# GpSimd multiplies the dense stage's products by the gates from the fourth pair of tiles on

## The chip, the cores and the metric

The kernel runs on one core of a Trainium2 chip. Its time is the device time of that core in microseconds. The core has five engines with a queue of their own: TensorE (PE, the matmuls; its weight loads are shown as PEld), VectorE (DVE), ScalarE (ACT), GpSimd (POOL) and SyncE (SP, which issues DMAs here). They meet only at semaphores, and each works through its own instructions in order.

## The reference, cut to what matters

One layer of a decoder: attention and a short convolution, then a mixer over 16384 experts of one neuron each. Only the mixer (`_peer`) is touched. For each of 512 tokens it picks 8 x 16 experts by key scores, and then:

```
ug = take(u, experts)                     # 128 rows of 2048 per token
vg = take(v, experts)
act = gelu(einsum("tkd,td->tk", ug, h)) * gates
out = einsum("tk,tkd->td", act, vg)
```

All is float32.

## The kernel before, in words

The 512 tokens are four blocks of 128. For block 0 the kernel gathers the chosen rows of u and v. For blocks 1, 2 and 3 it computes gelu(u h) for all experts (the sweep, 128 tiles of 128 experts) and keeps the products in HBM. The gates of blocks 2 and 3 are scattered into the same HBM array, so that `grid` holds for each expert 256 products and beside them 256 gates, which are zero where a token did not choose the expert.

The stage that follows the sweep, called the dense stage here, does two things at once.

- **The dense sum, blocks 2 and 3.** For each tile of 128 experts PE multiplies the weighed products by the tile of v. Both are float32 and split into a high and a low part, so a tile is 24 matmuls of 128x512. Tiles go in pairs: `grid_rows` holds four tiles (two pairs) and there are two such buffers. For a pair, VectorE multiplies products by gates in place (`weigh_pair`, L1930, one 128x512 instruction), ScalarE makes the high part (`split_pair`, L1346), VectorE the low part (`rest_pair`, L1935). For a tile, ScalarE makes the high part of v (`split_v`, L1342) and VectorE the low part (`rest_v`, L1925). PE waits for `v_lo_ready` at each tile and for `a_lo_ready` at each even one.
- **The gathered sum, block 1.** For each of 128 slots c GpSimd gathers one row of v per token into one of eight buffers (`gather_v`, L986), an indirect DMA of 1 MB, and VectorE adds it with its factor (`accumulate`, L1974). From slot 8 on the gather waits until sum c-7 is done (sum c-3 for the last eight: `LATE_AHEAD`). The factors of a head (16 slots) come from 16 tiny indirect DMAs (`fetch_product`, L975), issued one head ahead.

The order on the two engines is written out by hand. VectorE at tile n: `rest_v(n)`; at even n `weigh_pair(n//2+1)`; at odd n `rest_pair(n//2+1)`; then the sums `added(n)` to `added(n+1)`, which is 16 sums in 15 tiles from tile 7 on. GpSimd: the 16 fetches of head 0, the gathers of slots 2 to 7, and then for each head h eight gathers (slots 8 to 15 of the head) with two fetches for head h+1 behind each, followed by the first eight gathers of head h+1 with nothing between. Head 7 has no fetches. ScalarE at tile b: `split_v(b)`, and at odd b `split_pair` of the next pair behind it.

The line of before's `dense` that the change takes out, with its neighbours:

```
rest_v(tile, b)
if tile < TILES - 2 and b % 2 == 0:
    weigh_pair(pair + 1)
if tile < TILES - 2 and b % 2 == 1:
    rest_pair(pair + 1)
for c in range(added(tile), added(tile + 1)):
    accumulate(c)
```

Of the kernel before, what the change touches and what calls it, by code (L numbers as in the profile page):

```python
# [30 lines left out]
ALU = mybir.AluOpType  # L31
# [20 lines left out]
TOPK = 16  # L52
SWEPT = SEQ - P
SWEPT_BLOCKS = TB - 1
TILES = N_EXPERTS // P
# [11 lines left out]
PAIRS = TILES // 2  # L67
GROUP = 4
GROUP_RING = 2
FIRST_ADDED = 7  # L70
LATE_AHEAD = RING // 2
QUAD = 32
QUADS = P // QUAD
NEAR, FAR = 0, 1
# [117 lines left out]
def decoder_layer(nc, x, attn_norm_g, w_in, q_norm_g, k_norm_g, lambda_q1, lambda_k1, lambda_q2, lambda_k2,  # L192
                  subln_g, conv_w, w_out, ffn_norm_g, peer_w_q, peer_subkeys, peer_u, peer_v, out):
    ctx = ExitStack()
    with ctx:
        def sb(name, shape, dt=F32):
            return ctx.enter_context(nc.sbuf_tensor(name, shape, dt))

        def sem(name):
            return ctx.enter_context(nc.semaphore(name))  # L200

        def sems(name, n):
            return [sem(f"{name}{i}") for i in range(n)]
# [16 lines left out]
        def at(name, kb, shape, dt=F32):  # L220

            return nc.alloc_sbuf_tensor_at(name, shape, dt, offset=base + int(kb * KB))
# [37 lines left out]
        far_rows = at("far_rows", 128, [P, D])  # L260
        far_turned = at("far_turned", 136, [P, QUADS, KT, QUAD])
        v_row = [at(f"v_row{i}", 120 + 8 * i, [P, D]) for i in range(2)]
# [36 lines left out]
        def late_sb(name, shape, dt=F32):  # L299
# [5 lines left out]
        seg_rows = [nc.alloc_sbuf_tensor_at("near_rows", [P, D], F32, offset=late), far_rows]  # L305
        seg_turned = [nc.alloc_sbuf_tensor_at("near_turned", [P, QUADS, KT, QUAD], F32, offset=late + 8 * KB), far_turned]
        half_rows = [nc.alloc_sbuf_tensor_at(f"half_rows{i}", [P, D // HALVES], F32, offset=late + 4 * KB * i) for i in range(2)]
        half_rows.append(at("half_rows2", 124, [P, D // HALVES]))
        half_turned = [nc.alloc_sbuf_tensor_at(f"half_turned{i}", [P, QUADS, KT // HALVES, QUAD], F32,
                                               offset=late + 8 * KB + 4 * KB * i) for i in range(2)]  # L310
        half_turned.append(at("half_turned2", 140, [P, QUADS, KT // HALVES, QUAD]))
        wo0_hi = nc.alloc_sbuf_tensor_at("wo0_hi", [P, QUARTER, CHUNK], F32R, offset=late)
# [36 lines left out]
        pair = sb("pair", [P, 2, TOPK], U32)  # L349
# [24 lines left out]
        def pair_of(pair, first):  # L374

            half = pair % (GROUP // 2)
            return grid_rows[pair // (GROUP // 2) % GROUP_RING][:, 2 * half:2 * half + 2, first:first + GRID]

        def products_of(pair):
            return pair_of(pair, 0)  # L380

        def gates_of(pair):
            return pair_of(pair, GRID)
# [20 lines left out]
        ps_key_scores = [ps[:, 7 - c, :].rearrange("p (t n) -> p t n", t=TB) for c in range(2)]  # L404
        uT_rows = [u_tile[b][:, :].rearrange("p (a k e) -> p k a e", a=QUADS, e=QUAD) for b in range(2)]
        ps_uT = [ps[:, 2 * i:2 * i + 2, :].rearrange("p b (k e) -> p (b k) e", k=4) for i in range(2)]
# [97 lines left out]
        v_tile_used = sem("v_tile_used")  # L504
        group_in = sems("group_in", GROUP_RING)
        weights_ready = sem("weights_ready")
        a_hi_ready = sem("a_hi_ready")
        a_lo_ready = sem("a_lo_ready")
        dense_done = sem("dense_done")
# [38 lines left out]
        def halves_turned(j, i):  # L548

            return 4 * (NEAR_HEADS + 1) + 2 * (HALVES_A_HEAD * j + i)  # L550

        @nc_block.sync
        def _(sp):
# [15 lines left out]
            def next_half(j, i):  # L570

                (tile, _), half = half_place(j, i)
                sp.wait_ge(seg_ready[NEAR], halves_turned(j, i) - 2 * TURNED_SINCE[i])
                load_half(half_of_head(i), tile, half)
# [264 lines left out]
        def _(pool):  # L839
# [88 lines left out]
            def slot(t, h, s):  # L928
                return bass.IndirectOffsetOnAxis(ap=experts[:, t, h * TOPK + s:h * TOPK + s + 1], axis=0)
# [19 lines left out]
            for i in range(PEER_HEADS):  # L949
                pool.wait_ge(chosen, TB * i + 1)  # L950
                for b in range(TOPK):
                    c = TOPK * i + b
# [8 lines left out]
                    for h, n in scatters_beside(c):  # L961
                        if n == 0:
# [7 lines left out]
                            in_=gates[:, 2 + d, col:col + 1], in_offset=None, compute_op=ALU.add)\  # L970
                            .then_inc(grid_done, 16)

            def fetch_product(h, s):
                col = h * TOPK + s
                pool.indirect_dma_start(  # L975
                    out=dots[:, s:s + 1], out_offset=None, in_=products_one,
                    in_offset=bass.IndirectOffsetOnAxis(ap=cells[:, col:col + 1], axis=0))\
                    .then_inc(cells_in, 16)

            def gather_v(h, s):  # L980
                c = h * TOPK + s
                ahead = RING if c < TILES - RING else LATE_AHEAD
                if c >= RING:
                    pool.wait_ge(v_used, c - ahead + 1)
                    pool.sem_inc(past_wait, 1)
                pool.indirect_dma_start(out=v_ring[s % RING][:, :], out_offset=None, in_=v_table,  # L986
                                        in_offset=slot(1, h, s)).then_inc(v_in[s % RING], 16)
# [8 lines left out]
            for s in range(TOPK):  # L996
                fetch_product(0, s)
            for s in range(2, RING):
                gather_v(0, s)
            for h in range(PEER_HEADS):  # L1000
                if h < PEER_HEADS - 1:
                    pool.wait_ge(acts_ready, h + 1)
                for s in range(RING, TOPK):
                    gather_v(h, s)
                    if h < PEER_HEADS - 1:
                        fetch_product(h + 1, 2 * (s - RING))
                        fetch_product(h + 1, 2 * (s - RING) + 1)
                if h < PEER_HEADS - 1:
                    for s in range(RING):
                        gather_v(h + 1, s)  # L1010

        @nc_block.scalar
        def _(act):
# [327 lines left out]
                nc.scalar.activation(v_hi[b % 2][:, :], v_raw(h, b), ACT.Copy).then_inc(v_hi_ready, 1)  # L1342

            def split_pair(pair, i):
                act.wait_ge(weights_ready, pair + 1)
                nc.scalar.activation(a_hi[i % 2][:, :, :], products_of(i), ACT.Copy).then_inc(a_hi_ready, 1)  # L1346

            split_u(0, 0, 0)
# [33 lines left out]
        def _(dve):  # L1382
# [476 lines left out]
            def dot(c):  # L1859
                b = c % TOPK  # L1860
                dve.wait_ge(u_in[c % 2], 16 * (c // 2 + 1))
                v.tensor_tensor_reduce(out=u_row[c % 2][:, :], in0=u_row[c % 2][:, :], in1=h_rows[:, 0, :],  # L1862
                                       scale=1.0, scalar=0.0, op0=ALU.mult, op1=ALU.add,
                                       accum_out=dots0[:, b:b + 1]).then_inc(u_used[c % 2], 1)

            def add(c):
                b = c % TOPK
                dve.wait_ge(acts0_done, c + 1)
                dve.wait_ge(v0_in[c % 2], 16 * (c // 2 + 1))
                past()  # L1870
                v.scalar_tensor_tensor(out=x_rows[:, 0, :], in0=v_row[c % 2][:, :], scalar=acts0[:, b:b + 1],  # L1871
                                       in1=x_rows[:, 0, :], op0=ALU.mult, op1=ALU.add)\
                    .then_inc(v0_used[c % 2], 1)
                dve.wait_ge(v0_used[c % 2], c // 2 + 1)
# [48 lines left out]
            def rest_v(c, b):  # L1923
                dve.wait_ge(v_hi_ready, c + 1)
                v.tensor_tensor(v_lo[b % 2][:, :], v_raw(c // TOPK, b), v_hi[b % 2][:, :].bitcast(F32),  # L1925
                                ALU.subtract).then_inc(v_lo_ready, 1)

            def weigh_pair(pair):
                dve.wait_ge(group_in[pair // 2 % GROUP_RING], 16 * (pair // 2 // GROUP_RING + 1))
                v.tensor_tensor(products_of(pair), products_of(pair), gates_of(pair), ALU.mult)\  # L1930
                    .then_inc(weights_ready, 1)

            def rest_pair(pair):
                dve.wait_ge(a_hi_ready, pair + 1)
                v.tensor_tensor(a_lo[pair % 2][:, :, :], products_of(pair), a_hi[pair % 2][:, :, :].bitcast(F32),  # L1935
                                ALU.subtract).then_inc(a_lo_ready, 1)
# [37 lines left out]
                v.scalar_tensor_tensor(out=x_one[:, :], in0=v_ring[s % RING][:, :], scalar=acts[:, s:s + 1],  # L1974
                                       in1=x_one[:, :], op0=ALU.mult, op1=ALU.add).then_inc(v_used, 1)

            def added(tile):
                return min(TILES, max(0, (tile - FIRST_ADDED) * TILES // (TILES - 1 - FIRST_ADDED)))

            def dense():  # L1980
                rest_v(1, 1)
                dot(TILES - 1)
                rest_v(2, 2)
                rest_pair(1)
                add(TILES - 1)
                weigh_pair(2)
                for tile in range(3, TILES):
                    pair, b = tile // 2, tile % TOPK
                    rest_v(tile, b)
                    if tile < TILES - 2 and b % 2 == 0:  # L1990
                        weigh_pair(pair + 1)
                    if tile < TILES - 2 and b % 2 == 1:
                        rest_pair(pair + 1)
                    for c in range(added(tile), added(tile + 1)):
                        accumulate(c)
# [376 lines left out]
```

## Time and profile before

| | us |
|---|---|
| median of 3 runs (2933.47 to 2937.99) | 2937.51 |
| the profiled execution | 2933.1 |
| its span, first to last instruction | 2931.0 |
| PE busy in the span | 2879.4 |
| VectorE busy | 2392.2 |
| GpSimd busy | 1672.4 |
| ScalarE busy | 1057.1 |

The span is one execution. The dense stage's matmuls begin at 2184.1 us of it and end a few us before the last instruction. Busy time of an engine is an average over stages; what a change in one stage is worth is read in that stage. A POOL row of an indirect DMA is GpSimd's work to issue it, not the transfer. DMA share is the mean busy share of 16 DMA engines; it can read slightly over 1.

### The profile page before, as it was taken

To read this page: it belongs to the slowest core of one execution; us is meant where nothing else is said; L and a number is where in the kernel's file an instruction comes from. 1 tells how busy PE (TensorE), PEld (TensorE's weight loads), DVE (VectorE), ACT (ScalarE), POOL (GpSimd) and SP (SyncE) were. 2 spreads that over 40 slices of the span, in tenths; PEclk is the share of its full clock that TensorE was granted. 3 is DMA by queue.
4 is the path that set the end of the run, shared out by engine and by line. 5 is a ranking of instruction groups with operands and counts; after the bars stand their busy time and mean duration, and the time that the engine had idled before them with its cause. 6 is when DMAs were issued, how large, how long until landed. Compare 5 with 4: busy or idle time off the path is not lost.

```text
span 2931.0 us, 40438 instructions
## 1 busy us (share of the span) xinstructions
PE 2879.4 (98%) x14769; PEld 2546.0 (87%) x14769; DVE 2392.2 (82%) x3106; ACT 1057.1 (36%) x1375; POOL 1672.4 (57%) x1078
## 2 busy tenths in 40 slices
PE   7999999999999999999999999999999999999999
PEld 6888777778899999999999999999997777877787
DVE  6555888855679898988989898899777998999898
ACT  4121433341334343434333343444233333333333
POOL 1000565500116778765766666576868888887762
PEclk9999999999999999999999999999999999999999
DMA  8998999979978998999999999999999999999999
GB/s 300 328 354 275 307 307 297 302 277 335 308 261 304 328 355 307 347 322 342 335 314 348 310 341 329 332 341 365 335 367 394 411 419 416 418 421 419 419 416 375
DMA packets 332718, 1010.00 MB, mean 345 GB/s; under 512 B 65748, under 2 KB 182496, under 8 KB 247072
## 3 DMA queue, kind: packets, MB, share of 16 engines
q1 hardware_dynamic: 181648, 523.28, 48.0%
q0 software_dynamic: 113344, 454.44, 42.8%
q10 hardware_dynamic: 37584, 30.43, 3.2%
q8 instruction: 84, 1.38, 0.2%
q14 instruction: 58, 0.48, 0.0%
HBM read 881.01 MB, written 127.01 MB: 344 GB/s over the span
## 4 chain that ended last, share of the span: by engine, by line
PE 68%; DVE 11%; issue 6%; DMA 6%; POOL 6%; ACT 1%; ACTq 0%; DVEq 0%; SPq 0%; POOLq 0%
PE ps L2026 21%; PE ps L2028 21%; PE ps L2027 21%; POOL dots L975 4%; DMA v_ring<-in_peer_v,experts 4%; DVE x_rows L1871 2%; PE ps L2267 2%; POOL v_ring L986 2%; DVE x_one L1974 2%; DMA v_two<-in_peer_v 1%; DVE v_lo L1925 1%; DVE uT_lo L1835 1%; DVE u_row L1862 1%; PE ps L2109 1%; DMA wc_raw<-in_w_in 1%
## 5 line engine op out<-in xcount | busy, mean ns | idle before, releaser
L2026 PE MATMUL ps<-hT_hi,uT_hi 128*128 128x384 f32 x2048 | 697.3, 340 | 5.2 <-DVE uT_lo L1830 2.3
L2028 PE MATMUL ps<-h2T_lo,uT_hi 128*128 128x384 f32 x2048 | 686.0, 335 | 0.0
L2027 PE MATMUL ps<-hT_hi,uT_lo 128*128 128x384 f32 x2048 | 685.0, 334 | 0.0
L967 POOL DMA_INDIRECT grid<-gates,grid_cells x256 | 547.6, 2139 | 81.9 <-issue 81.9
L2026 PE MATMUL ps<-v_hi,a_hi 128*128 128x512 f32 x1024 | 407.4, 398 | 23.1 <-DVE v_lo L1925 22.3
L2027 PE MATMUL ps<-v_hi,a_lo 128*128 128x512 f32 x1024 | 404.8, 395 | 0.0
L2028 PE MATMUL ps<-v_lo,a_hi 128*128 128x512 f32 x1024 | 404.8, 395 | 0.0
L1342 ACT ACTIVATE v_hi<-v_two 128x2048 fp32r<-128x2048 f32 x126 | 241.6, 1918 | 447.4 <-PE ps L2028 376.0
L2026 PEld LDWEIGHTS ps<-hT_hi,uT_hi 128*128 128x128 f32 x2048 | 384.6, 188 | 17.3 <-DVE uT_lo L1835 6.5
L2027 PEld LDWEIGHTS ps<-hT_hi,uT_lo 128*128 128x128 f32 x2048 | 384.8, 188 | 1.9
L2028 PEld LDWEIGHTS ps<-h2T_lo,uT_hi 128*128 128x128 f32 x2048 | 384.3, 188 | 0.0
L986 POOL DMA_INDIRECT v_ring<-in_peer_v,experts x128 | 289.0, 2258 | 106.5 <-DVE x_one L1974 72.1
L1925 DVE TENSOR_TENSOR v_lo<-v_two,v_hi 128x2048 fp32r<-128x2048 f32 x126 | 288.4, 2289 | 52.2 <-ACT v_hi L1342 45.2
L1974 DVE SCALAR_TENSOR_TENSOR x_one<-v_ring,acts,x_one 128x2048 f32<-128x2048 f32 x128 | 300.3, 2346 | 19.6 <-DMA v_ring<-in_peer_v,experts 17.4
L975 POOL DMA_INDIRECT dots<-products_one,cells x128 | 280.9, 2194 | 42.9 <-issue 38.7
L1871 DVE SCALAR_TENSOR_TENSOR x_rows<-v_row,acts,x_rows 128x2048 f32<-128x2048 f32 x128 | 300.1, 2345 | 4.4 <-ACT acts L1279 2.7
L1862 DVE CUSTOM_DVE_ANT_0 u_row<-u_row,h_rows 128x2048 f32<-128x2048 f32 x128 | 292.6, 2287 | 4.3 <-DMA u_row<-in_peer_u,experts 3.1
L939 POOL DMA_INDIRECT u_row<-in_peer_u,experts x128 | 190.9, 1492 | 166.8 <-DVE dots L1862 109.4
L946 POOL DMA_INDIRECT v_row<-in_peer_v,experts x128 | 163.8, 1279 | 210.9 <-DVE x_rows L1871 157.0
L2026 PEld LDWEIGHTS ps<-v_hi,a_hi 128*128 128x128 f32 x1024 | 194.1, 190 | 76.3 <-DVE v_lo L1925 19.4
L2026 PE MATMUL ps<-w_hi,hT_hi 128*128 128x512 f32 x624 | 244.2, 391 | 1.2 <-DVE wi_lo L1419 1.2
L2027 PE MATMUL ps<-w_hi,hT_lo 128*128 128x512 f32 x624 | 243.5, 390 | 0.0
(210 smaller groups left out, 4957.0 us busy)
## 6 DMA issues: line engine op xcount, KB each, us to landing
v_two<-in_peer_v SPq DMA_DIRECT2D x63, 2048.0 KB
u_tile<-uT_all SPq DMA_DIRECT2D x70, 1024.0 KB
u_tile<-in_peer_u SPq DMA_DIRECT2D x58, 1024.0 KB
grid_rows<-grid SPq DMA_DIRECT2D x32, 1024.0 KB
half_rows<-in_peer_u SPq DMA_DIRECT2D x58, 512.0 KB, 7.2
uT_all<-half_turned POOLq DMA_DIRECT2D x232, 128.0 KB, 5.0
near_rows<-in_peer_u SPq DMA_DIRECT2D x25, 1024.0 KB, 8.2
uT_all<-near_turned SPq DMA_DIRECT2D x100, 256.0 KB, 7.0
```

What stands on the lines that cost most here:

```text
L939: pool.indirect_dma_start(out=u_row[c % 2][:, :], out_offset=None, in_=u_table, in_offset=slot(0, c // TOPK, c % TOPK)).then_inc(u_in[c % ...
L967: pool.indirect_dma_start(out=grid, out_offset=bass.IndirectOffsetOnAxis(ap=grid_cells[:, d, col:col + 1], axis=0), in_=gates[:, 2 + d, co ...
L975: pool.indirect_dma_start(out=dots[:, s:s + 1], out_offset=None, in_=products_one, in_offset=bass.IndirectOffsetOnAxis(ap=cells[:, col:col ...
L986: pool.indirect_dma_start(out=v_ring[s % RING][:, :], out_offset=None, in_=v_table, in_offset=slot(1, h, s)).then_inc(v_in[s % RING], 16)
L1342: nc.scalar.activation(v_hi[b % 2][:, :], v_raw(h, b), ACT.Copy).then_inc(v_hi_ready, 1)
L1862: v.tensor_tensor_reduce(out=u_row[c % 2][:, :], in0=u_row[c % 2][:, :], in1=h_rows[:, 0, :], scale=1.0, scalar=0.0, op0=ALU.mult, op1=ALU ...
L1871: v.scalar_tensor_tensor(out=x_rows[:, 0, :], in0=v_row[c % 2][:, :], scalar=acts0[:, b:b + 1], in1=x_rows[:, 0, :], op0=ALU.mult, op1=ALU ...
L1925: v.tensor_tensor(v_lo[b % 2][:, :], v_raw(c // TOPK, b), v_hi[b % 2][:, :].bitcast(F32), ALU.subtract).then_inc(v_lo_ready, 1)
L1974: v.scalar_tensor_tensor(out=x_one[:, :], in0=v_ring[s % RING][:, :], scalar=acts[:, s:s + 1], in1=x_one[:, :], op0=ALU.mult, op1=ALU.add) ...
L2026: mm(out, a_hi, b_hi, start=first, stop=False)
L2027: mm(out, a_lo, b_hi, start=False, stop=False)
L2028: return mm(out, a_hi, b_lo, start=False, stop=last)
```

## The change

The instruction of `weigh_pair` is the same, on the same operands. For pairs 0, 1 and 2 VectorE still issues it. For pairs 3 to 63, 61 in all, GpSimd does, signals a new semaphore `pool_weighed`, and `split_pair` on ScalarE waits for that. On GpSimd the instruction stands ahead of a gather's wait: before the gather that waits for the sum numbered `sums`, all pairs up to tile//2+1 are weighed, where tile is the tile at which VectorE does that sum. So the last pair weighed is the one that VectorE weighed in that same tile before. It also stands at the start of each head, and at the end.

```
+WEIGHED_BY_DVE = 3
+        pool_weighed = sem("pool_weighed")
 (GpSimd)
+            def weigh_pair(pair):
+                pool.wait_ge(group_in[pair // 2 % GROUP_RING], 16 * (pair // 2 // GROUP_RING + 1))
+                nc.gpsimd.tensor_tensor(products_of(pair), products_of(pair), gates_of(pair), ALU.mult)\
+                    .then_inc(pool_weighed, 1)
+            weighed = [WEIGHED_BY_DVE]
+            def weigh_ahead(sums):
+                tile = next(n for n in range(FIRST_ADDED, TILES) if added(n + 1) >= sums)
+                while weighed[0] < PAIRS and weighed[0] <= tile // 2 + 1:
+                    weigh_pair(weighed[0])
+                    weighed[0] += 1
 ...
                 if c >= RING:
+                    weigh_ahead(c - ahead + 1)
                     pool.wait_ge(v_used, c - ahead + 1)
 ...
             for h in range(PEER_HEADS):
+                weigh_ahead(TOPK * h + 1)
                 if h < PEER_HEADS - 1:
                     pool.wait_ge(acts_ready, h + 1)
 ...
+            weigh_ahead(TILES)
 (ScalarE, split_pair)
-                act.wait_ge(weights_ready, pair + 1)
+                if isinstance(pair, int) and pair < WEIGHED_BY_DVE:
+                    act.wait_ge(weights_ready, pair + 1)
+                else:
+                    act.wait_ge(pool_weighed, pair - WEIGHED_BY_DVE + 1)
 (VectorE, dense)
-                    if tile < TILES - 2 and b % 2 == 0:
-                        weigh_pair(pair + 1)
```

`added` moves to where both engines' programs can call it.

## Rows read from the trace of the kernel before

**Rows 1.** Windows: length; busy PE, PEld, DVE, ACT, POOL; PEclk, DMA share, GB/s.
```profile
2250.00:2300.00 50.00, 50.00 (x218) 40.75 (x217) 46.51 (x28) 19.33 (x13) 44.30 (x19) 1.00 1.00 405
...
2700.00:2750.00 50.00, 44.99 (x194) 35.67 (x192) 41.96 (x24) 19.33 (x13) 37.23 (x18) 1.00 1.01 415
```

**Rows 2.** DMA view, 2300 to 2800 us: total, then the gathers' issue to landing.
```profile
DMA packets 25481, 209.38 MB, mean 419 GB/s; under 512 B 5415, under 2 KB 5415, under 8 KB 5415
...
v_ring<-in_peer_v,experts POOLq DMA_INDIRECT x94, 29.2
```

**Rows 3.** VectorE's multiplications, first and last of 54, 2223 to 2838 us (timeline).
```profile
2223.79 0.68 DVE L1930 TENSOR_TENSOR grid_rows<-grid_rows 128x512 f32<-128x512 f32 x1
...
2837.11 0.68 DVE L1930 TENSOR_TENSOR grid_rows<-grid_rows 128x512 f32<-128x512 f32 x1
```

**Rows 4.** Groups of instructions by line, 1650 to 2931 us: busy, mean ns, idle before.
```profile
L1974 DVE SCALAR_TENSOR_TENSOR x_one<-v_ring,acts,x_one 128x2048 f32<-128x2048 f32 x128 | 300.3, 2346 | 19.6 <-DMA v_ring<-in_peer_v,experts 17.4 <-DVE acts L1959 1.6
L986 POOL DMA_INDIRECT v_ring<-in_peer_v,experts x128 | 289.0, 2258 | 106.5 <-DVE x_one L1974 72.1 <-issue 34.4
L1925 DVE TENSOR_TENSOR v_lo<-v_two,v_hi 128x2048 fp32r<-128x2048 f32 x126 | 288.4, 2289 | 52.2 <-ACT v_hi L1342 45.2 <-issue 6.0
...
L975 POOL DMA_INDIRECT dots<-products_one,cells x128 | 280.9, 2194 | 42.9 <-issue 38.7 <-DMA grid<-products 4.2
...
L1930 DVE TENSOR_TENSOR grid_rows<-grid_rows 128x512 f32<-128x512 f32 x64 | 43.8, 684 | 3.8 <-DMA grid_rows<-grid 3.8
...
L1346 ACT ACTIVATE a_hi<-grid_rows 128x512 fp32r<-128x512 f32 x64 | 39.3, 614 | 8.4 <-DVE grid_rows L1930 4.9 <-issue 2.2 <-DVE dots L1862 1.2
```

**Rows 5.** Waits, 1680 to 2931 us: total, times, longest.
```profile
POOL v_ring L986 <- DVE x_one L1974: 72.1, 15, 22.2
...
PE ps L2026 <- DVE v_lo L1925: 22.3, 17, 5.4
```

**Rows 6.** GpSimd's timeline: start, length, instruction, idle before it.
```profile
2206.45 0.94 POOL L975 DMA_INDIRECT dots<-products_one,cells  x1 [0.30 <-issue]
...
2403.45 1.90 POOL L986 DMA_INDIRECT v_ring<-in_peer_v,experts  x1 [0.30 <-issue]
2405.66 2.56 POOL L986 DMA_INDIRECT v_ring<-in_peer_v,experts  x1 [0.30 <-issue]
2408.53 1.91 POOL L975 DMA_INDIRECT dots<-products_one,cells  x1 [0.30 <-issue]
```

**Rows 7.** VectorE's timeline beside the last three.
```profile
2402.26 2.28 DVE L1925 TENSOR_TENSOR v_lo<-v_two,v_hi 128x2048 fp32r<-128x2048 f32 x1
...
2405.06 2.35 DVE L1974 SCALAR_TENSOR_TENSOR x_one<-v_ring,acts,x_one 128x2048 f32<-128x2048 f32 x1
2407.32 2.29 DVE L1925 TENSOR_TENSOR v_lo<-v_two,v_hi 128x2048 fp32r<-128x2048 f32 x1
```

**Rows 8.** Timeline: low part of pair 3; PE's first matmul of tile 6; gather 7.
```profile
2214.90 0.68 DVE L1935 TENSOR_TENSOR a_lo<-grid_rows,a_hi 128x512 fp32r<-128x512 f32 x1
...
2224.87 0.40 PE L2026 MATMUL ps<-v_hi,a_hi 128*128 128x512 f32 x1
...
2230.43 2.91 POOL L986 DMA_INDIRECT v_ring<-in_peer_v,experts  x1 [0.30 <-issue]
```

**Rows 9.** Timeline: low parts of pairs 5 and 16; gathers 9 and 32.
```profile
2240.43 0.68 DVE L1935 TENSOR_TENSOR a_lo<-grid_rows,a_hi 128x512 fp32r<-128x512 f32 x1
2241.64 2.55 POOL L986 DMA_INDIRECT v_ring<-in_peer_v,experts  x1 [0.30 <-issue]
...
2364.05 0.68 DVE L1935 TENSOR_TENSOR a_lo<-grid_rows,a_hi 128x512 fp32r<-128x512 f32 x1
2384.48 2.18 POOL L986 DMA_INDIRECT v_ring<-in_peer_v,experts  x1 [0.31 <-issue]
```

**Rows 10.** GpSimd's groups in the whole span: two that read SBUF.
```profile
L865 POOL TENSOR_TENSOR qk_ss<-qk_ss,minus_half 128x16 f32<-128x16 f32 x8 | 23.2, 2902 | 271.8 <-DVE qk_ss L1565 271.8
...
L853 POOL TENSOR_SCALAR_AFFINE_SELECT alibi<-alibi 128x512 f32<-128x512 f32 x1 | 0.6, 612 | 0.0
```

More of the change, by code:

```diff
@@ L550, in halves_turned, with added @@
             return 4 * (NEAR_HEADS + 1) + 2 * (HALVES_A_HEAD * j + i)
+        def added(tile):
+            return min(TILES, max(0, (tile - FIRST_ADDED) * TILES // (TILES - 1 - FIRST_ADDED)))
         @nc_block.sync
@@ L1975, in accumulate @@
                                        in1=x_one[:, :], op0=ALU.mult, op1=ALU.add).then_inc(v_used, 1)
-            def added(tile):
-                return min(TILES, max(0, (tile - FIRST_ADDED) * TILES // (TILES - 1 - FIRST_ADDED)))
             def dense():
```

## The prediction

> **What bounds the kernel now.** The change touches only the dense stage, so the windows of that stage come first. In a quiet window PE is busy 50.00 of 50 us and the DMA share is 1.00; in the worst, PE is busy 44.99 and the DMA share still 1.01 [rows 1]. Two things are thus near their end: PE and the DMA engines. The DMA view prices the second. In 500 us 209.38 MB moved, 419 GB/s [rows 2]. VectorE's multiplications, one a pair, give the pace of the stage: 54 of them from 2223.79 to 2837.11 us, 53 steps in 613.3 us, 11.57 us a pair of tiles [rows 3]. In 11.57 us 419 GB/s moves 4.85 MB; a pair needs 2.10 MB of v, 0.52 of grid and 2.13 gathers of 1.05 MB, 4.86 MB in all. So the stage runs on average at the rate of its transfers, and PE's idle time before v_lo, 22.3 us in 17 waits [rows 5], is mostly what is left over where they come late.
>
> VectorE comes third, with 46.51 of 50 us busy [rows 1]. The groups show what it does: a v_lo of 2.289 us a tile, a sum of 2.346 us, and the two small instructions of a pair (0.684 us the one that moves) [rows 4]. GpSimd is fourth on paper, 44.30 us busy [rows 1], but with 0.3 us of issue ahead of each DMA it is all but full: in that window 19 x 0.3 = 5.7 us beside 44.3 is the whole window. Its long rests, 72.1 us before gathers, of which one is 22.2 [rows 5], lie mainly after head 6, when no fetches are left. So the change takes 61 x 0.684 = 41.7 us from an engine with a little room and puts a longer instruction on one that has none.
>
> **What GpSimd's durations are made of.** This decides the sum. With nothing in its way an indirect DMA takes GpSimd 0.94 us, and the next starts 0.30 us later [rows 6]. Beside a busy VectorE it takes 1.90 to 2.56, and its end is tied to VectorE: v_lo ends at 2404.54 and GpSimd's row at 2405.35; the sum ends at 2407.41, GpSimd at 2408.22; v_lo ends at 2409.61, GpSimd at 2410.44 [rows 6, 7]. That is 0.8 us behind the end of one of VectorE's long instructions, three times of three, and 200 of the 211 issues over 1.5 us between 2230 and 2840 us stand so. GpSimd's read of its indices waits until VectorE's running instruction is over. It gets one of them for each long VectorE instruction (4.13 a pair: two v_lo, 2.13 sums), and one per 1.24 us while VectorE stands still.
>
> This is what the Trainium skill states (SBUF — State Buffer, Who interferes with whom): an instruction of VectorE with two SBUF inputs and a GpSimd instruction that reads SBUF exclude each other for the whole of one of them. By that rule the multiplication on GpSimd also holds VectorE up for its own length, and moving work between these two engines frees less than it seems. The trace agrees on GpSimd's side; it has no case of the other.
>
> **Price of one multiplication on GpSimd.** No two-input 128x512 multiplication is in GpSimd's rows. From below there is one input over 128x512, 0.612 us; from above a power over 128x16, 2.902 us [rows 10]. I take 1.2, twice the first for two inputs, since it is nearest in shape, and keep both ends.
> By the Trainium skill (GPSIMD Engine Reference, Performance versus the Vector engine) a two-input instruction takes 1.96 times VectorE's time; an estimate from that page and 0.684 us is 1.34 us, 4 us more over the stage than the sum below.
>
> **Where it stands on GpSimd.** VectorE needs pair k's high part for its low part one tile after the old multiplication. What matters is when GpSimd comes past the new place. Pair 5 is weighed ahead of gather 9, which stands at 2241.64, while VectorE took the low part of pair 5 at 2240.43: 1.2 us late. Pair 16 stands ahead of gather 32, at 2384.48, and its low part was taken at 2364.05: 20.4 us late [rows 9]. Reading all pairs so, the lateness rises in each half of a head that has fetches, from about 0 to 12 to 20 us, and falls again in the half that has none. Before, eight buffers of gathers covered that swing. Now a pair's multiplication is queued behind the gathers and fetches, and VectorE can't pass the odd tile without it. GpSimd's fetches are 16 a head, all in one half.
>
> **The sum, in steps.**
> 1. *Entry.* Pair 3's low part was taken at 2214.90; GpSimd reaches the first place, the start of head 0, only after gather 7, which ends at 2230.43 + 2.91 = 2233.3 [rows 8]. VectorE stops at 2215 for want of it, and then GpSimd's last six gathers take 1.24 each: it is there at about 2228.9. Pair 3 and pair 4 are weighed, 3's high part takes 0.6 [rows 4], ScalarE's v_hi of tile 6 stands behind it, then v_lo: PE begins tile 6 at about 2235 instead of 2224.87 [rows 8]. +10 us.
> 2. *Halves with fetches*, seven (heads 0 to 6), 3.75 pairs each. VectorE needs for a pair 2 x 2.21 + 2.13 x 2.27 (start to start) + 0.60 = 9.9 us. GpSimd has 8 x 3 / 3.75 = 6.4 DMAs and one multiplication. It gets 4.13 of them beside VectorE's long instructions, and one more runs while the high part is made after the multiplication. The rest falls into a stop of VectorE before the low part: the issue caught at the end of v_lo (1.2), 1.27 more x 1.24 (1.6), the multiplication with its issue (1.5), high part and semaphores (1.0): 5.3 us. So 15.2 us a pair against 11.57: +3.6 x 26.25 = +95 us. Each half begins with a lead that GpSimd regained, some 3 us by the order of one gather and one wait for VectorE: -21. Together +74 us.
> 3. *Halves without fetches.* GpSimd has 2.13 gathers and one multiplication a pair and keeps up. VectorE needs 9.9 plus 1.2 in which the multiplication holds it: 11.1, under the 11.57 of the transfers. 0. If the multiplication took 2.9 us, it would be 12.8, +1.2 x 26.75 = +33.
> 4. *VectorE's 41.7 us.* Hidden: the transfers set 11.57 a pair before as after where GpSimd keeps up. 0; at most the 5 to 10 us of PE's larger gaps that a late VectorE caused.
> 5. *Tail.* After the last fetch GpSimd waits for sums, and its multiplication fits into those waits (the 22.2 us one [rows 5] among them). 0.
>
> Sum: 10 + 74 = +84 us on 2933.1, 3017. The median of the runs lies 4.4 above that execution: 3021. In the stops PE's clock may fall as in other gaps, but PE needs only some 11 of 15.2 us there.
>
> Ends: a multiplication of 0.61 us gives 0.6 less a pair in step 2, -16 us; one of 2.9 gives +45 in step 2 and +33 in step 3, +162 in all. A lead of 8 us instead of 3, half a ring of slack, gives -35.
>
> **Rivals.**
> - *The lateness is paid once.* VectorE is pushed back by the greatest lateness, about 20 us, in the first head, and from there GpSimd stands early enough for all later ones. For it: the lateness returns to about 0 before each half. Against it: the new place is tied to a sum seven slots back, so GpSimd cannot run further ahead. Time: 10 + 20 + nothing more: 2937.5 + 30 = 2967.
> - *GpSimd's multiplication is much dearer* (it waits for VectorE a whole long instruction, and is itself near the 2.9 us). +130 to +160: 3080.
> - *The other side.* VectorE, relieved of 0.34 us a tile, reaches v_lo earlier, its small waits vanish and GpSimd catches up in VectorE's idle time, which grows by 41.7 us; 41.7 us of it hold 34 issues of 1.24 us. It decides if GpSimd's place comes before VectorE's need, that is if the lateness above were below zero; then up to 15 of PE's 22.3 us come back: 2922. Against it: 18 us of lateness at entry, where VectorE is half idle anyhow.
> - *No change:* the stops lie beside the DMA engines' backlog and PE never sees them. Against it: v_lo has two buffers, some 5 us of cover, less than each stop in step 2 adds up to over a half.
>
> **Chances.** The forecast (steps 1 and 2) 0.65; paid once 0.14; much dearer 0.11; faster 0.06; no change 0.04. The likeliest is 3021. The range takes in the smaller price with the larger lead (3021 - 51 = 2970) and most of the dearer case: 2960 to 3075. Two tenths of a per cent, some 6 us, is what a measurement can tell from no change. Faster 0.06, same 0.04, slower 0.90.
>
> **What would show it.** In the profile after: GpSimd's 61 multiplications near 1.2 us each with a wait for VectorE ahead or inside; v_hi or a_hi on ScalarE waiting for GpSimd's multiplication, some 4 us a pair in the halves with fetches, and VectorE's low part waiting for a_hi; PE's idle time before v_lo grown from 22 to about 100 us; the DMA share below 0.9 in those halves; issues of 0.94 us more frequent; VectorE waiting no longer for gathered rows (17.4 us before [rows 4]). Wrong if GpSimd's multiplication shows as early as VectorE's did, if a pair in a half with fetches takes under 13 us, or if later heads show no stops.

## The result and the profile after

The changed kernel takes 3012.39 us (median of 4 runs, 3010.86 to 3013.65), the kernel before in the same runs 2935.89: a ratio of 1.0261 (95% interval 1.0249 to 1.0274), 76.5 us slower. The forecast was 3021, +84.

The page of the changed kernel, span and busy time of the engines, which answers to the table of before:

```profile
span 3009.1 us, 40432 instructions
...
PE 2904.6 (97%) x14769; PEld 2557.9 (85%) x14769; DVE 2372.6 (79%) x3045; ACT 1060.4 (35%) x1375; POOL 1692.5 (56%) x1139
```

GpSimd has 61 instructions more, VectorE 61 fewer, and neither engine's busy time moved by more than some 20 us. TensorE's grew by 25.2 us on the same matmuls, and its idle time by the rest of the 78 us of span. What it waits for stands in the waits of 1680 to 3010 us (total, times, longest; before in [rows 5]):

```profile
ACT a_hi L1373 <- POOL grid_rows L982: 244.1, 57, 16.1
POOL v_ring L1008 <- DVE x_one L2001: 123.5, 30, 24.7
...
DVE a_lo L1962 <- ACT a_hi L1373: 115.6, 29, 14.0
...
PE ps L2048 <- DVE v_lo L1952: 74.0, 43, 9.1
```

ScalarE's high part waits for GpSimd's multiplication 57 times, VectorE's low part for the high part, and PE for v_lo: 74.0 us against 22.3.

That wait is 51.7 of the 76.1 us by which the dense stage's matmuls last longer (743.6 us before, 819.7 after). Most of the rest is TensorE's clock. After the change 182 of the 3071 steps from one of these matmuls to the next take 0.3 to 0.6 us instead of 0.23; before, 66 do. The first window of [rows 1], after:

```profile
2250.00:2300.00 50.00, 45.69 (x190) 36.19 (x188) 35.92 (x20) 17.78 (x13) 42.88 (x23) 0.97 0.86 334
```

In the seven halves with fetches the granted clock is 0.94 to 0.97, where it was 1.00 before in six of them and 0.94 in the last. TensorE still rests there, 6.1 of 55.5 us between pairs 12 and 16, so it is not what sets the pace of these halves. No run isolates the clock; the run below that keeps only the place loses 25.4 us with a mean granted clock of 0.996, the same as before.

The groups of 1650 to 3009 us (busy, mean ns, idle before), against [rows 4]:

```profile
L2001 DVE SCALAR_TENSOR_TENSOR x_one<-v_ring,acts,x_one 128x2048 f32<-128x2048 f32 x128 | 311.3, 2432 | 3.5 <-DVE acts L1986 2.2 <-DMA v_ring<-in_peer_v,experts 0.3
L1952 DVE TENSOR_TENSOR v_lo<-v_two,v_hi 128x2048 fp32r<-128x2048 f32 x126 | 294.2, 2336 | 35.7 <-ACT v_hi L1366 29.4 <-issue 6.1
...
L982 POOL TENSOR_TENSOR grid_rows<-grid_rows 128x512 f32<-128x512 f32 x61 | 110.7, 1818 | 1.0
```

VectorE's waits for gathered rows went from 17.4 us to 0.3. Its own instructions grew: sums from 2.346 to 2.432 us in the mean, v_lo from 2.289 to 2.336. Of GpSimd's 61 multiplications 36 are recorded with 1.27 to 1.31 us and 25 with 2.51 to 2.59.

**A half of a head with fetches**, timeline of GpSimd, then VectorE, then ScalarE (start, length, idle before):

```profile
2355.90 1.30 POOL L982 TENSOR_TENSOR grid_rows<-grid_rows 128x512 f32<-128x512 f32 x1
2357.37 0.97 POOL L1008 DMA_INDIRECT v_ring<-in_peer_v,experts  x1 [0.16 <-issue]
2358.64 3.06 POOL L996 DMA_INDIRECT dots<-products_one,cells  x1 [0.30 <-issue]
2362.00 1.88 POOL L996 DMA_INDIRECT dots<-products_one,cells  x1 [0.30 <-issue]
2364.18 1.96 POOL L1008 DMA_INDIRECT v_ring<-in_peer_v,experts  x1 [0.30 <-issue]
2366.45 1.90 POOL L996 DMA_INDIRECT dots<-products_one,cells  x1 [0.30 <-issue]
2368.65 0.94 POOL L996 DMA_INDIRECT dots<-products_one,cells  x1 [0.30 <-issue]
2369.61 1.31 POOL L982 TENSOR_TENSOR grid_rows<-grid_rows 128x512 f32<-128x512 f32 x1
```

```profile
2358.52 2.34 DVE L2001 SCALAR_TENSOR_TENSOR x_one<-v_ring,acts,x_one 128x2048 f32<-128x2048 f32 x1
2360.78 2.28 DVE L1952 TENSOR_TENSOR v_lo<-v_two,v_hi 128x2048 fp32r<-128x2048 f32 x1
2362.98 2.34 DVE L2001 SCALAR_TENSOR_TENSOR x_one<-v_ring,acts,x_one 128x2048 f32<-128x2048 f32 x1
2365.25 2.28 DVE L1952 TENSOR_TENSOR v_lo<-v_two,v_hi 128x2048 fp32r<-128x2048 f32 x1
2371.61 0.69 DVE L1962 TENSOR_TENSOR a_lo<-grid_rows,a_hi 128x512 fp32r<-128x512 f32 x1 [4.09 <-ACT a_hi L1373]
```

```profile
2370.95 0.64 ACT L1373 ACTIVATE a_hi<-grid_rows 128x512 fp32r<-128x512 f32 x1 [8.56 <-POOL grid_rows L982]
```

GpSimd rests only for the issue between its instructions, and the period from one multiplication to the next is 13.71 us. VectorE ends v_lo at 2367.5 and stands 4.1 us: GpSimd ends one fetch 0.8 us after v_lo, issues the next in 0.30 + 0.94, multiplies in 1.31, ScalarE takes 0.64.

**A half without fetches**, VectorE and then GpSimd:

```profile
2404.09 2.35 DVE L2001 SCALAR_TENSOR_TENSOR x_one<-v_ring,acts,x_one 128x2048 f32<-128x2048 f32 x1
2406.36 3.38 DVE L1952 TENSOR_TENSOR v_lo<-v_two,v_hi 128x2048 fp32r<-128x2048 f32 x1
```

```profile
2402.79 2.22 POOL L1008 DMA_INDIRECT v_ring<-in_peer_v,experts  x1 [3.34 <-DVE x_one L2001]
2405.02 2.57 POOL L982 TENSOR_TENSOR grid_rows<-grid_rows 128x512 f32<-128x512 f32 x1
```

The multiplication is recorded with 2.57 us: it waits for the sum's end at 2406.4 and then runs to 2407.59. v_lo has the same start as the sum's end but takes 3.38 us instead of 2.28. That is the hold: 1.1 us, inside VectorE's own record and not in its idle time. Of the 256 v_lo and sums of the stage 14 are recorded with more than 2.6 us, 16.3 us over their usual lengths together. None of them lies in one of the 27 pairs of halves with fetches counted below. The longest is at pair 57, beside three multiplications in a row:

```profile
2911.63 6.40 DVE L2001 SCALAR_TENSOR_TENSOR x_one<-v_ring,acts,x_one 128x2048 f32<-128x2048 f32 x1 [0.29 <-DVE acts L1986]
```

```profile
2912.09 3.78 POOL L982 TENSOR_TENSOR grid_rows<-grid_rows 128x512 f32<-128x512 f32 x3
```

The steps between the low parts of successive pairs (VectorE's a_lo, starts read from both timelines) are a clock for the stage. Their sums, after minus before:

```
                                        pairs   before, mean   after - before
entry, pairs 3 to 5                         3       12.56           +10.0
halves with fetches                        27       11.13           +70.7
pairs with three sums (12, 19, ..., 57)     7       14.57            -4.6
halves without fetches                     18       11.10            -1.7
tail, pairs 58 to 63                        6       11.08            +0.6
```

That is +75.0 of the 78.1 us between the spans; 3.1 lie ahead of pair 2's low part, where nothing was changed and other runs scatter as much.

### The profile page after: what moved, and what is told of

Its sections match the earlier page's. It is cut to its first block, busy times and chain, and to the rows that moved or that the text cites. A ratio compares the mean times of both kernels' runs of the same rounds, so it can differ in the third digit from the quotient of the medians.

```text
span 3009.1 us, 40432 instructions
## 1 busy us (share of the span) xinstructions
PE 2904.6 (97%) x14769; PEld 2557.9 (85%) x14769; DVE 2372.6 (79%) x3045; ACT 1060.4 (35%) x1375; POOL 1692.5 (56%) x1139
## 4 chain that ended last, share of the span: by engine, by line
PE 63%; DVE 12%; POOL 11%; issue 8%; DMA 3%; ACT 2%; ACTq 0%; DVEq 0%; SPq 0%; POOLq 0%
PE ps L2048 20%; PE ps L2050 19%; PE ps L2049 19%; POOL dots L996 7%; DVE x_rows L1898 2%; DVE x_one L2001 2%; POOL v_ring L1008 2%; PE ps L2289 2%; DVE v_lo L1952 2%; POOL grid_rows L982 1%; DVE uT_lo L1862 1%; DVE u_row L1889 1%; DVE uT_lo L1857 1%; PE ps L2131 1%; DMA wc_raw<-in_w_in 1%
## 5 line engine op out<-in xcount | busy, mean ns | idle before, releaser
L974 POOL DMA_INDIRECT grid<-gates,grid_cells x256 | 540.6, 2112 | 83.3 <-issue 83.3
L2048 PE MATMUL ps<-v_hi,a_hi 128*128 128x512 f32 x1024 | 417.6, 408 | 74.6 <-DVE v_lo L1952 74.0
L2050 PE MATMUL ps<-v_lo,a_hi 128*128 128x512 f32 x1024 | 412.3, 403 | 0.0
L2049 PE MATMUL ps<-v_hi,a_lo 128*128 128x512 f32 x1024 | 411.8, 402 | 0.0
L1008 POOL DMA_INDIRECT v_ring<-in_peer_v,experts x128 | 243.3, 1901 | 156.9 <-DVE x_one L2001 123.5
L2001 DVE SCALAR_TENSOR_TENSOR x_one<-v_ring,acts,x_one 128x2048 f32<-128x2048 f32 x128 | 311.3, 2432 | 3.5 <-DVE acts L1986 2.2
L996 POOL DMA_INDIRECT dots<-products_one,cells x128 | 243.4, 1902 | 42.2 <-issue 38.7
L2048 PE MATMUL ps<-w_hi,hT_hi 128*128 128x512 f32 x624 | 244.1, 391 | 1.7 <-DVE wi_lo L1446 1.5
## 6 DMA issues: line engine op xcount, KB each, us to landing
v_two<-in_peer_v SPq DMA_DIRECT2D x63, 2048.0 KB, 11.2
```

The source lines that it names most:

```text
L974: pool.indirect_dma_start(out=grid, out_offset=bass.IndirectOffsetOnAxis(ap=grid_cells[:, d, col:col + 1], axis=0), in_=gates[:, 2 + d, co ...
L996: pool.indirect_dma_start(out=dots[:, s:s + 1], out_offset=None, in_=products_one, in_offset=bass.IndirectOffsetOnAxis(ap=cells[:, col:col ...
L2048: mm(out, a_hi, b_hi, start=first, stop=False)
L2049: mm(out, a_lo, b_hi, start=False, stop=False)
L2050: return mm(out, a_hi, b_lo, start=False, stop=last)
```

## The experiments

Q is the theory of the prediction: the place in GpSimd's queue behind gathers and fetches. P is the port: what a multiplication holds VectorE up. O: a lateness paid once. Each figure is against the kernel before in the same runs.

**VectorE keeps pairs 3 and 4.**

```
-WEIGHED_BY_DVE = 3
+WEIGHED_BY_DVE = 5
 (VectorE, dense)
+                    if b % 2 == 0 and pair + 1 < WEIGHED_BY_DVE:
+                        weigh_pair(pair + 1)
```

> The changed kernel, but VectorE keeps pairs 3 and 4 as well; GpSimd multiplies from pair 5 on, 59 times. Theory Q (queue: the loss is the place of the multiplications behind GpSimd's gathers and fetches, and GpSimd's lack of time in the halves of a head that have fetches): the 9.1 us gap of TensorE at tile 6 goes and nothing takes its place, so 9 to 10 us less than the changed kernel, about +67 us on before. Rival P (port: the loss is what each GpSimd multiplication holds VectorE up): two of 61 go, 2 to 3 us less, about +74. Rival O (once: a lateness paid once at the first multiplication and never again): the loss moves to pair 5 and stays whole, +76.

3001.84 against 2935.23, 1.0225 (1.0207 to 1.0243): +66.6, as Q has it: 9.9 us less than the changed kernel. By the clock pairs 3 to 5 shrink by 6.8 of these and the time ahead of pair 2 by 2.9; the later groups stay within 1 us.

**No fetches for heads 1 to 7, after and before.**

```
-                    if h < PEER_HEADS - 1:
-                        fetch_product(h + 1, 2 * (s - RING))
-                        fetch_product(h + 1, 2 * (s - RING) + 1)
```

> The changed kernel without the fetches of products for heads 1 to 7 (112 small indirect DMAs on GpSimd left out; block 1 uses head 0's products throughout). All 61 multiplications stay on GpSimd. Q: no half has more than 8 gathers and 4 multiplications, so GpSimd keeps up; what is left over its twin without the change is the entry, +9 to +15 us. P: each multiplication still holds VectorE up, so +55 to +70 over the twin stays. O: the twin plus 20 to 30.

> The twin of the run before: the kernel before without the fetches of heads 1 to 7. If the stage runs at the rate of its transfers and of TensorE, the fetches were hidden and this is 0 to 15 us under before (VectorE's 17 us of waits for gathered rows may go). If GpSimd's issue time bounded the kernel before, it is 25 us or more under it.

2952.14 and 2926.32 against 2935.23 (1.0048, 1.0029 to 1.0066; 0.9962, 0.9948 to 0.9976). The change costs 25.8 us without the fetches and 76.5 with them: 50.7 us need the fetches. P's 55 to 70 fails as the whole cause, but Q's 9 to 15 is short as well; with the entry off, some 16 us remain. Here VectorE works beside the multiplications: 30 of its long instructions are recorded with more than 2.6 us, 33.7 us over their usual lengths together. So the port has a part. The fetches of before were nearly hidden (-8.9).

**Only the place.** GpSimd signals from the places, VectorE multiplies.

```
-                nc.gpsimd.tensor_tensor(products_of(pair), ...).then_inc(pool_weighed, 1)
+                pool.sem_inc(pool_weighed, 1)
```

> VectorE does all multiplications at their old places; GpSimd does none, but signals at the place where the changed kernel has each, and ScalarE's high part waits for both. Only the place is kept, no port and no duration of a multiplication. Q: entry 7 us, and in a half with fetches 6.4 DMAs a pair still stand ahead of the signal: 1.5 us a pair less than the changed kernel and 0.6 more for VectorE's own multiplication, so some 24 us less than the changed kernel, +50 on before (35 to 60). P: no loss, within 6 us of before. O: +10 to +20.

2935.32 against 2935.23, 0.9998 (0.9989 to 1.0008). No loss, and it looked like P. But the waits of this run name no wait of ScalarE for GpSimd (the three longest are shown), where the changed kernel has 244.1 us:

```profile
ACT v_hi L1364 <- PE ps L2049: 402.0, 113, 12.2
POOL v_ring L1006 <- DVE x_one L1998: 73.4, 16, 22.2
DVE v_lo L1949 <- ACT v_hi L1364: 48.4, 78, 7.8
```

```
+                pool.memset(alibi[:, pair:pair + 1], 0.0).then_inc(pool_weighed, 1)
```

 Q, if the sequencer ran ahead in the run before: the place alone costs, entry some 7 us and most of the stops in halves with fetches, +35 to +60 on before. If the place costs nothing in itself (P): within 6 us of before.

2959.69 against 2934.32, 1.0092 (1.0071 to 1.0112): +25.4, and the waits are back:

```profile
ACT a_hi L1370 <- POOL alibi L981: 152.2, 29, 16.8
DVE a_lo L1959 <- ACT a_hi L1370: 69.5, 28, 14.1
```

The place alone costs, but 10 us less than Q's lower figure; a pair in the middle of a half with fetches takes 11.96 us, against 13.70 with the multiplication.

**A short multiplication at the place** (32 of 512 columns):

```
-  products_of(pair), products_of(pair), gates_of(pair)
+  products_of(pair)[:, :, 0:16], products_of(pair)[:, :, 0:16], gates_of(pair)[:, :, 0:16]
```

> The changed kernel, but GpSimd's multiplication covers only 16 of 256 columns of each tile (32 of 512 a pair; the rest of the products stays unweighed). Place, waits and port lock stay, the length falls from 1.3 us to some 0.2 to 0.4. Q: 1.0 us less in each of 26 pairs of halves with fetches, 26 us less than changed, +50 on before. P: with the hold of 1.1 us on VectorE gone almost nothing is left, +15 or less.

2961.91, 1.0086 (1.007 to 1.0103): +27.6. Both totals were missed, Q's by 22 and P's by 13. A pair in a half with fetches takes 12.67 us, 1.03 less than 13.70, just as Q has it. The total fell by 49 and not by 26, because the pairs with three sums and those just behind a half with fetches shrank as well (11.47 to 10.43, 14.05 to 12.55).

**The length without the reading.** Two fills of 128x512 instead of the multiplication.

```
+                for n in range(2):
+                    pool.memset(alibi[:, :], 0.0).then_inc(pool_weighed, 1)
```

> The changed kernel with each multiplication on GpSimd replaced by two fills of 128x512 of an unused tile (0.6 us each by the nearest row, a mask over 128x512, 0.61 us); they only write, so they have the length and the place of the multiplication but read nothing through the port shared with VectorE. The products stay unweighed. Q: in halves with fetches VectorE stands still during the multiplication anyway, so 13.7 us a pair stays, and the total is within 15 us of the changed kernel, +60 to +76 on before. P: the hold is the loss, so it falls to the +25 of the run that keeps only the place.

2992.2 against 2936.19, 1.0196 (1.0175 to 1.0217): +56.0. Both fills took 1.12 us together, and VectorE's instructions are back at their old lengths (groups, 2180 to 2990 us):

```profile
L2004 DVE SCALAR_TENSOR_TENSOR x_one<-v_ring,acts,x_one 128x2048 f32<-128x2048 f32 x128 | 300.4, 2347 | 3.4 <-DVE acts L1989 2.2
L1955 DVE TENSOR_TENSOR v_lo<-v_two,v_hi 128x2048 fp32r<-128x2048 f32 x126 | 288.4, 2290 | 46.1 <-ACT v_hi L1369 45.8
...
L986 POOL MEMSET alibi<- 128x512 f32 x122 | 65.3, 535 | 3.9
```

A pair in a half with fetches still takes 13.51. So reading through the shared port is worth at most some 20 us of the 76.5 (76.5 - 56.0). By the clock the change takes 16.2 us more than the fills: 9.8 in the seven pairs with three sums, 3.4 in the halves without fetches, 1.0 in the tail, 4.3 in the 27 pairs with fetches, and 2.3 less at the entry. The 4.3 are the fills being 0.2 us shorter. What is left, some 12 us, lies where the hold meets a working VectorE: the port is worth 12 to 20 us. Q's 60 to 76 missed by 4, P's +25 by 31.

**Fetches spread over 12 gathers instead of 8, after and before.**

```
+            def spread_over(place):
+                if place < 4: return (2 * place, 2 * place + 1)
+                return (4 + place,) if place < 12 else ()
```

> The changed kernel with each head's 16 fetches spread over 12 gathers (four with two, eight with one) instead of over 8 with two each. Same instructions in number. Q: a pair has 4.3 DMAs and one multiplication instead of 6.4 and one, so the stops of VectorE shrink: 11.2 to 12.4 us a pair in all halves, +20 to +55 on before. P: the number of holds is the same, +70 to +76.

> The kernel before with the same spread of the fetches. If the fetches of before hide behind transfers and TensorE, -10 to +3 us; the kernel without them was 9 us faster, so no more than that can come.

After: 2992.71 against 2934.32, 1.0197 (1.0178 to 1.0214), +58.4, a little over Q's range and under P's; pairs with two fetches a gather still take 13.70, those with one 11.46. Before: 2951.49, 1.0056 (1.0037 to 1.0075), +17.2, and the expectation missed. Against this twin the change costs 41.2 us and not 76.5. VectorE waits for the last fetches at the start of a head, 8.68 us here:

```profile
2324.21 0.17 DVE L1967 TENSOR_TENSOR acts<-dots,gates 128x16 f32<-128x16 f32 x1 [8.68 <-DMA dots<-products_one,cells]
```

**GpSimd multiplies only in halves without fetches**, 31 pairs.

```
+        def by_pool(pair):
+            c = place_of(pair)
+            return pair >= 5 and (c % TOPK < RING or c >= TILES - RING)
```

> GpSimd multiplies only the 31 pairs whose place lies in a half without fetches (and in the tail), VectorE the other 33, pairs 3 and 4 among them; ScalarE's dense loop is written out so that it can wait for either. Q: GpSimd keeps up in these halves, so nothing of the +76 is left but the lead of pairs that follow a half with fetches, -2 to +8 us on before. P: 31 of 61 holds, +35 to +40.

3004.85 against 2936.19, 1.0237 (1.0222 to 1.0251): +68.7. Both expectations fail. The clock has one step of 21.1 to 22.5 us in each of seven heads (pairs 9, 16, 24, 31, 39, 46, 54), the first that GpSimd takes after a half with fetches. VectorE there, and GpSimd:

```profile
2295.35 0.69 DVE L1980 TENSOR_TENSOR a_lo<-grid_rows,a_hi 128x512 fp32r<-128x512 f32 x1 [10.29 <-ACT a_hi L1391]
```

```profile
2292.41 0.94 POOL L1025 DMA_INDIRECT v_ring<-in_peer_v,experts  x1 [0.30 <-issue]
2293.38 1.27 POOL L998 TENSOR_TENSOR grid_rows<-grid_rows 128x512 f32<-128x512 f32 x1
```

What GpSimd falls behind while VectorE runs freely is paid at once at the first multiplication behind it. Q's "it keeps up there" was wrong for the first pair of such a half, though [rows 9] had shown it 20 us behind at pair 16.

**The multiplications one pair further ahead** (pairs 3 and 4 with VectorE).

```
-                while weighed[0] < PAIRS and weighed[0] <= tile // 2 + 1:
+                while weighed[0] < PAIRS and weighed[0] <= tile // 2 + 2:
```

> The run in which VectorE keeps pairs 3 and 4, and each GpSimd multiplication stands one pair of tiles (11 us) further ahead among the gathers. Q, with GpSimd idle in halves without fetches: the lead taken there absorbs up to 11 us of the four stops of 2.65 us in each half with fetches, so +5 to +25 instead of +67, unless the grid rows have not landed yet, in which case GpSimd stands before its gathers and it is worse. P: the number of holds is the same and each is now beside a working VectorE: +60 or more.

2984.73 against 2936.19, 1.0166 (1.0151 to 1.0181): +48.5. One pair of lead saves 18 of 66.6 us. Both expectations missed: P's by 11, Q's by 24. The backlog of a half is nearer 20 us than 11, so the later stops stay at 4.1 us each. And the port costs more here: where the stops are gone VectorE works beside the multiplications, and 35 of its long instructions are recorded with more than 2.6 us, 44.8 us over their usual lengths together, against 16.3 in the change.

**GpSimd multiplies only where it is on time.** 14 pairs.

```
+            return pair in (12, 19, 27, 34, 41, 42, 49) or pair >= 57
```

> GpSimd multiplies only the 14 pairs 12, 19, 27, 34, 41, 42, 49 and 57 to 63, the ones at whose place it stood in the trace of before at most about 1 us after VectorE's need, or had rested; VectorE does the other 50. Q with backlog (what GpSimd is behind at the first multiplication after a half with fetches is paid there, 10 to 11 us a head): here it has caught up, so no stop of 10 us anywhere; what stays is the hold of VectorE in pairs with three sums, about 1 us each, and some 3 us at pair 57: +2 to +10 on before. If every multiplication cost the same (76 us over 61), +18.

2939.31 against 2935.02, 1.0016 (1.0007 to 1.0025): +4.3, in Q's range. Fourteen at an equal price would be +18. No version here in which GpSimd multiplies beats the kernel before.

## Why the prediction came out

- **The bound.** Half right. VectorE's relief brought nothing, as said. But the reason given, transfers at 11.57 us a pair, is not what the clock shows: pairs of the kernel before take mostly 10.9 or 11.2 us, those with three sums 13.1, and three take 17.2, 14.6 and 17.8 (27, 42, 49). 11.57 is the mean of these. The 10.9 to 11.2 are TensorE's own pace: a pair is 48 matmuls, and in a window in which it never rests 218 of them take 50 us [rows 1], 11.0 us a pair. After the change the halves without fetches run at 10.6 to 11.5 with a DMA share of 0.88 to 0.97, so the transfers don't hold them there.
- **Step 1, entry.** Right: PE's first matmul of tile 6 at 2235.29, forecast 2235. The rows of GpSimd and PE:

```profile
2228.21 0.94 POOL L1008 DMA_INDIRECT v_ring<-in_peer_v,experts  x1 [0.30 <-issue]
2229.18 2.49 POOL L982 TENSOR_TENSOR grid_rows<-grid_rows 128x512 f32<-128x512 f32 x2
```

```profile
2235.29 0.80 PE L2048 MATMUL ps<-v_hi,a_hi 128*128 128x512 f32 x1 [9.12 <-DVE v_lo L1952]
```

- **Step 2, halves with fetches.** Right in mechanism: +70.7 against +74. That the size is so near is luck: its terms were off in opposite ways. The stop was put at 5.3 us and is 4.1: 6 DMAs a pair and not 6.4 (the third sum falls into pairs of another kind), no issue time ahead of the multiplication, 0.7 instead of 1.0 for the high part. A pair takes 13.7, not 15.2, some 39 us less over the halves. Against that, the pairs took 11.13 before and not 11.57, 12 us more; and the lead of 21 us in all that was subtracted did not come back as such, for the first pairs of a half take 13.0 to 15.1.
- **Step 3.** The price 1.2 us was near (1.30 with VectorE at rest). That a hold costs nothing there was wrong: the fills show 12 to 20 us for the reading, mostly in pairs with three sums, where VectorE has no slack.
- **Step 4.** The three late pairs of before went (17.2, 14.6 and 17.8 became 14.1, 14.1 and 12.9, 8.6 us), inside the 5 to 10 given as the most, but not by VectorE's relief. They go as well where VectorE multiplies every pair and a fill of one column keeps the place (13.1, 13.1 and 13.3), and in the kernel before without fetches (13.1, 13.1 and 12.9). In all three runs VectorE waits at most 0.5 us in all for gathered rows, against 17.4 before. The gain about cancelled the hold, which the sum had at nothing; that, too, is luck.
- **Step 5, tail.** 0 forecast; 3.5 us at pair 57 (13.09 to 16.54), where the three multiplications in a row hold VectorE's sum, and 0.6 behind it.
- **Rivals.** *Paid once* falls: stops stand in every head. *Much dearer* falls: 1.30 us. *The other side* and *no change* fall. Of the signs named, most came: the waits of ScalarE and VectorE, more issues under 1.1 us (78 against 29 from 2180 us on), no wait of VectorE for gathered rows. Two came short: PE's idle time before v_lo is 74.0 us and not about 100, and the DMA share of the seven halves with fetches is 0.92 to 0.98 and not below 0.9 (0.86 in the window shown above). In the DMA view of 2300 to 2800 us gathers land sooner, 10.1 us after the issue (29.2 before [rows 2]):

```profile
DMA packets 22993, 189.44 MB, mean 379 GB/s; under 512 B 4881, under 2 KB 4881, under 8 KB 4881
...
v_ring<-in_peer_v,experts POOLq DMA_INDIRECT x84, 10.1
```

The ladder of runs, each against before: place only +25.4; place with a short reading multiplication +27.6; place with the length +56.0; the change +76.5. Place and length in a full queue are worth some 25 to 30 us each, the port 12 to 20. The steps are not strictly additive: VectorE multiplies in the first run and in none of the others.

## What to carry to other kernels

An engine that is 57% busy in the page can be full in the stage that counts. Before work is moved to it, find in the old trace when it comes past the new place and when the result is needed; that difference, pair by pair, told here which multiplications were free (14 for 4 us) and which were not. What mattered most was the backlog at that moment. Where the stops were gone the port took over as a cost, so a lead alone did not bring the time back (+48.5 with one pair of lead).

## What the runs showed of the hardware

- The exclusion works both ways, so these two engines meet at more than semaphores. GpSimd's issue of an indirect DMA ends 0.8 us after VectorE's running two-input instruction, and GpSimd's two-input multiplication stretches VectorE's next one from 2.28 to 3.38 us. The stretch is recorded as busy time of the stretched engine, so no wait view names it. Beside fills, which only write, no v_lo or sum is recorded with over 2.6 us (2.347 and 2.290 us in the mean).
- A semaphore increment by GpSimd's sequencer was not held back by the DMAs in front of it: +0.1 us, against +25.4 with a fill of one column in its place.
- After 9.12 us of rest TensorE's next matmul is recorded with 0.80 us where the same one took 0.40 before [rows 8]. The granted clock of 2235 to 2239 us is 0.50, the lower of the two levels (1.2 GHz), and of 2242 to 2246 us 1.00 again.
- The 128x512 multiplication took 1.30 us on GpSimd and 0.684 on VectorE, 1.9 times.
